# Byte phases of weight slots and of the tiles streamed past them, in a two-block transformer kernel

## What is computed

```python
# first block, per layer
proj = x @ w_in                    # 1024 -> 3360 columns, split into 14 parts
ya = banded chunk attention        # 4 heads, relative bias
yb = latent attention              # low-rank q and kv, rope
yc = sliding window, sinks         # rope
ym = attention over a memory of 256 rows: mem @ w_mem_kv
x = layer_norm(alpha * x + (concat(y * silu(gate)) @ w_out))
# second block, per layer
p = rmsnorm(x) @ w_in
y_f = real(fft2(u)) @ w_f + b_f    # as products with cosine and sine tables
y_a = windowed attention(q, k, v, sink)
x = x + concat(rmsnorm(y_f), rmsnorm(y_a)) @ w_o
up = dwconv(rmsnorm(x) @ w_up)     # 1024 -> 2 * 2816, 3 taps
x = x + (silu(gate) * val) @ w_down
```

## The kernel before, in words

| tile | byte address | modulo 256 |
|---|---|---|
| w_hi, slots 0 and 1 | 16512, 24768 | 128, 192 |
| w_stage, slots 0 and 1 | 33024, 41280 | 0, 64 |
| w_lo, slots 0 and 1 | 49536, 57792 | 128, 192 |
| xt, xh, xl, g | 66048, 82432, 98816, 115200 | 0 |
| probs, probs_t, tmp, ident | 131584, 137728, 141824, 150016 | 0 |
| neg_max, row_sum, row_inv | 172960, 173024, 173088 | 160, 224, 32 |
| union (km, mix_h, act_h, u_h, pq_h) | 173376 | 64 |
| qa, lat_h; qb, mix_l, a_h; mem_h, act_l | 177472; 189760; 197952 | 64 |
| q2, k2, v2 | 198016, 206208, 208256 | 128 |

## Time and profile before

### The profile page before, as it was taken

One profiled execution on the slowest core, in us unless ns is written; L12 is line 12 of the kernel. 1 busy time (PEld: TensorE's weight loads), 2 busy tenths in 40 slices (PEclk: granted clock), 3 DMA queues, 4 the chain that ended last, 5 costly groups with the idle time before them and its releaser, 6 DMA issues.

```text
span 1707.0 us, 23556 instructions
## 1 busy us (share of the span) xinstructions
PE 1652.6 (97%) x8770; PEld 1323.7 (78%) x8770; DVE 777.3 (46%) x1428; ACT 697.0 (41%) x1152; POOL 676.1 (40%) x514
## 2 busy tenths in 40 slices
PE   7999899999999999999999999999999999999999
PEld 6876678787667778778888888887877788888887
DVE  7325564402656366653654035524675454304540
ACT  4445452534545254543443134333564443213331
POOL 3533206442420433535334444345344444444433
PEclk9999999999999989989999999999999999999999
DMA  7222113222210322113222232233221222222222
GB/s 272 100 75 70 57 34 141 90 84 77 69 57 26 112 74 82 60 41 101 96 98 74 98 103 95 71 112 121 75 76 50 99 98 92 76 103 99 98 90 83
DMA packets 26879, 150.69 MB, mean 88 GB/s; under 512 B 3888, under 2 KB 4144, under 8 KB 12912
## 3 DMA queue, kind: packets, MB, share of 16 engines
q1 hardware_dynamic: 23968, 142.78, 24.7%
q10 hardware_dynamic: 2832, 6.84, 1.1%
HBM read 142.66 MB, written 2.10 MB: 85 GB/s over the span
## 4 chain that ended last, share of the span: by engine, by line
PE 67%; issue 20%; POOL 9%; DVE 3%; DMA 1%; ACT 1%; POOLq 0%; ACTq 0%; DVEq 0%
PE ring L598 59%; POOL w_lo L578 9%; PE outs L670 2%; PE scores L650 1%; PE ring L650 1%; PE ring L693 1%; DMA xt<-in_x 1%; PE ring L679 1%; PE scores L679 1%; DVE probs_t L1630 0%; PE ring L727 0%; DVE xt L1805 0%; ACT w_hi L1135 0%; DVE row_sum L1671 0%; PE ring L1024 0%
## 5 line engine op out<-in xcount | busy, mean ns | idle before, releaser
L578 POOL TENSOR_TENSOR w_lo<-w_stage,w_hi 128x258 fp32r<-128x258 f32 (+6 forms) x478 | 653.8, 1397 | 1011.6 <-ACT w_hi L1135 600.7
L598 PE MATMUL ring<-xh,w_lo 128*128 128x512 f32 x1296 | 518.3, 400 | 28.5 <-DVE w_lo L1560 10.8
L598 PE MATMUL ring<-xh,w_hi 128*128 128x512 f32 x1296 | 513.5, 396 | 0.0
L598 PE MATMUL ring<-xl,w_hi 128*128 128x512 f32 x1296 | 512.9, 396 | 0.0
L598 PEld LDWEIGHTS ring<-xh,w_lo 128*128 128x128 f32 x1296 | 245.4, 189 | 92.7 <-issue 18.5
L598 PEld LDWEIGHTS ring<-xh,w_hi 128*128 128x128 f32 x1296 | 245.5, 189 | 55.5
L598 PEld LDWEIGHTS ring<-xl,w_hi 128*128 128x128 f32 x1296 | 245.9, 190 | 53.7
L1491 ACT ACTIVATE w_hi<-w_stage 128x2048 fp32r<-128x2048 f32 (+2 forms) x70 | 116.6, 1666 | 158.3 <-PE ring L598 158.3
L1501 ACT ACTIVATE g<-ring,convw 128x512 f32<-128x512 f32 x88 | 68.1, 778 | 245.5 <-DVE ring L2008 245.5
L1135 ACT ACTIVATE w_hi<-w_stage 128x2064 fp32r<-128x2064 f32 (+2 forms) x85 | 127.7, 1515 | 80.9 <-PE ring L598 70.6
L1990 DVE TENSOR_TENSOR xt<-xt,ring 128x512 f32<-128x512 f32 x48 | 33.0, 688 | 238.2 <-PE ring L598 238.2
(11 more groups left out here) (287 smaller groups left out, 2169.7 us busy)
## 6 DMA issues: line engine op xcount, KB each, us to landing
w_stage<-in_mixed SPq DMA_DIRECT2D x62, 1032.0 KB, 4.8
w_stage<-in_up SPq DMA_DIRECT2D x44, 1024.0 KB, 4.8
w_stage<-in_down SPq DMA_DIRECT2D x16, 768.0 KB, 4.2
w_stage<-in_down SPq DMA_DIRECT2D x16, 640.0 KB, 3.9
xt<-in_x ACTq DMA_DIRECT2D x4, 512.0 KB, 11.5
g<-q SPq DMA_DIRECT2D x16, 128.0 KB, 2.3
out_t<-xt ACTq DMA_DIRECT2D x8, 256.0 KB, 2.0
mem_f<-in_mem SPq DMA_DIRECT2D x1, 1024.0 KB, 9.7
```

The costliest lines, as they stand in the source:

```text
L578: ins = nc.gpsimd.tensor_tensor(w_lo[:, slot, cols], source[:, cols], w_hi[:, slot, cols].bitcast(F32), ALU.subtract)
L598: ins = nc.tensor.matmul(o, lhs, rhs, start=start, stop=stop, skip_group_check=True)
```

## The change

The weight slots get a pitch of 2112 floats (8448 bytes, 33 x 256) in w_hi and w_lo, and both tiles begin at a byte that is 192 modulo 256. w_stage keeps its pitch and is placed into the space behind w_hi's second slot. The space behind the second slot of w_lo is given back. xh is placed at 0 modulo 256 (xt, xh, xl and g are all multiples of 256 long), and union is rounded up to a multiple of 256. neg_max, row_sum and row_inv move into the 192 bytes between the slots of w_hi. Nothing else is changed: no instruction is added, removed or reordered.

```diff
 SLOT = 2 * 2 * 516
+PITCH = SLOT + 48
+LINES = 256
+W_PHASE = 192
...
-        def place(name, shape, dt, offset=None):
+        def place(name, shape, dt, offset=None, phase=None):
             size = int(np.prod(shape[1:])) * 4
+            if phase is not None:
+                at[0] += (phase - at[0]) % LINES
             where = at[0] if offset is None else offset
             if offset is None:
                 at[0] += -(-size // 32) * 32
             return nc.alloc_sbuf_tensor_at(name, shape, dt, offset=where)
 
-        w_hi = place("w_hi", [P, 2, SLOT], F32R)
-        w_stage = place("w_stage", [P, 2, SLOT], F32)
-        w_lo = place("w_lo", [P, 2, SLOT], F32R)
+        w_hi = place("w_hi", [P, 2, PITCH], F32R, phase=W_PHASE)
+        pad = at[0] - 4 * (PITCH + PITCH - SLOT)
+        w_stage = place("w_stage", [P, 2, SLOT], F32, at[0] - 4 * (PITCH - SLOT))
+        at[0] += 4 * (2 * SLOT - (PITCH - SLOT))
+        w_lo = place("w_lo", [P, 2, PITCH], F32R, phase=W_PHASE)
+        at[0] -= 4 * (PITCH - SLOT)
         xt = place("xt", [P, KD, TOK], F32)
-        xh = place("xh", [P, KD, TOK], F32R)
+        xh = place("xh", [P, KD, TOK], F32R, phase=0)
         xl = place("xl", [P, KD, TOK], F32R)
...
-        neg_max = place("neg_max", [P, 2, 8], F32)
-        row_sum = place("row_sum", [P, 2, 8], F32)
-        row_inv = place("row_inv", [P, 2, 8], F32)
+        neg_max = place("neg_max", [P, 2, 8], F32, pad)
+        row_sum = place("row_sum", [P, 2, 8], F32, pad + 64)
+        row_inv = place("row_inv", [P, 2, 8], F32, pad + 128)
...
         one_row = place("one_row", [P, 2], F32)
+        at[0] += -at[0] % LINES
         union = at[0]
```

## The result

The changed kernel took 1688.33 us, the median of 4 runs (1686.72 to 1693.39), against 1703.69 for the kernel before in the same comparison: a ratio of 0.9906, 95% interval 0.9876 to 0.9935. In a second comparison, with more runs, it was 1689.46 against 1706.07, ratio 0.9894, interval 0.987 to 0.9917. The forecast was 1690.3.

The account below looks back on a forecast made before the run. PE, busy 97% of the span, was taken as the bound, through its matmul pace. Terms summed to 14.0 us, less 1.0 gave 13 us (0.8%); from the median 1703.27 the forecast was 1690.3, range 1683 to 1699.

Parts of the forecast that it names:

- The reading of rows 5 to 7: Feed-forward matmuls: weights at 192 under a stream at 0 run at 229.1 ns, other pairs about 232.8, modulo 256.
- The first rival: Slot 1 is faster for something other than its phase, so both slots keep their times: 1703 us, chance 0.10.
- The sum of 14.0 us: Gains added over feed-forward projections, output projection, other xh and xl products, u tiles, and bounds for unknown families.
- 4.0 + 3.6: Slot-0 gains in us for products of xh and xl: 4.0 in the feed-forward up projection, 3.6 in the others.
- 22.0 instead of 22.4: Expected sign in the profile after: time in us for two chunks of the output projection.
- Only half of it: Rival: the pair (192, 0) is fast for xh but not act and mix; gain 7.5 us, 1695.8, chance 0.17.
- slower: Rival: distance counts over more than 256 bytes, so slot 1 loses its place: 1711.7 us, chance 0.05.
- The 1.0 us taken off for waits: Deduction from the attention stages' 4.5 us gain, for waits on DVE and ACT and stretches at half clock.
- The clock hides it. No case of its own.: Rival: half-clock time, 61 us over the span, spreads the runs; it only widens the range, with no separate chance.
- The rule against the change: The skill's claim that PE never waits on anyone: weight placement against the stream could cost nothing, ending at 1703 us.

Follow-up runs that it names:

- Weights alone: The changed kernel's weight placement (192 in both slots), with the union kept at 64 modulo 256: 1693.11 us against 1705.02 for the kernel before, ratio 0.9947.
- the union alone: The kernel before with only the union rounded up to 0 modulo 256, weights left at 128 and 192: ratio 1.0011 to the kernel before.
- everything by 64: The changed kernel with everything from w_hi on moved up by 64 bytes, weights at 0 and streams at 64: 1690.6 us, ratio 0.993.
- both slots at 128: The changed kernel with both weight slots at 128 instead of 192 modulo 256, streams at 0: 1714.75 us in one run.
- the seven distances above: Versions with stationary weight address minus stream address at 0, 32, 64, 128, 160, 192 (the change) or 224 modulo 256: 227.2 to 233.3 ns a matmul.

## Why the prediction was right

- *The reading of rows 5 to 7, that the pair of phases sets the pace.* Shown. Weights alone left act slow, the union alone made act's slot 1 fast, everything by 64 kept the pace, and both slots at 128 made slot 1 slow. The first rival (something else about slot 1) falls with the last of these.
- *The sum of 14.0 us.* The two traces give 14.0 and 14.4. In the first of them the products of xh and xl give 7.3 us where the sum has 4.0 + 3.6, the down projection 4.0 for 3.9, the output projection 1.3 for 1.6, the u tiles 1.0 for 0.9, and all the rest 0.4 for 0. The 1.6 was a little too high because I took the pace from ACT's rows: by PE's own starts it was 232.8 ns there, not 233.3. For the same reason the sign "22.0 instead of 22.4" didn't come (22.27), though the pace did.
- *"Only half of it" and "slower".* Both fall: act and mix reach 228.9 and 229.1 ns with their union at an odd multiple of 256, and slot 1 kept its 229. Steps of 256 showed no effect in any version here.
- *The 1.0 us taken off for waits.* Mis-sized: waits rose by 1.5 to 2.8 us, by the view of PE's waits 2.1 and 2.6. Of this, 1.4 us is the wait for a_l behind the one add of DVE above, and that belongs to the one profiled execution of before, which had the add short; it can hardly be put down to the change.
- *"The clock hides it. No case of its own."* That was the weak step. I took the clock as spread around an unchanged mean; on the same chip the mean rose by 0.0037, worth 5 to 7 us in the change's favour. With that known and the pace right, the forecast would have been 18 us or more. The waits, mis-sized the other way, bring it back towards the measured 15.4 and 16.6, so that 13 came this close, inside the range, is in part luck.
- *The rule against the change.* The Trainium skill, "SBUF — State Buffer", section "SBUF: two separate sides", has PE among those that "never wait on anyone". By that rule the seven distances above should have run alike; they differ by 2.7% in pace, from 227.2 to 233.3 ns. The measurement decides. What inside the chip makes the difference no run here shows.

## What to carry to other kernels

Where PE streams wide float32r matmuls back to back, compare the starts of successive matmuls by the buffer slot of the weights: a slot whose size isn't a multiple of 256 bytes runs the experiment on placement for you, and a difference there is a forecast. For streams of 512 columns, the address of the stationary operand minus that of the stream was best at 0 modulo 256 in pace and next at 192; the other five tried were slow. In time, distance 0 wasn't shown to be better than 192. Before promising the time, look at the granted clock of many runs on both sides, on one chip: here it was worth 5 to 7 us beside 14 of pace.

## What was not expected of the hardware

The best distance is 0 (227.2 ns), right beside slow ones at 32 and 224 (233.3), with 192 between them at 229.1; 256-column streams have another order. The mean granted clock differed between placements (0.9825 to 0.9890 in versions with the same instructions, run on one chip) and didn't simply follow how fast PE ran.
